# Later shifts, scales and gates beside the second norm, and another order of the exact split, in a two-model fp32 kernel

## The reference, cut to what matters

```python
mod = silu(c) @ ada_w[l] + ada_b[l]          # the same with c_ctx for the context
sh1, sc1, g1, sh2, sc2, g2 = split(mod, 6)
h = rmsnorm(x) * (1 + sc1) + sh1
x = x + g1 * mixer(h)                        # attention (and pooling) and an output projection
h2 = rmsnorm(x) * (1 + sc2) + sh2            # "the second norm"
x = x + g2 * hier_moe(h2)                    # 32 experts, top 2 inside one of 4 groups
```

## Time and profile before

| | us |
|---|---|
| median of three runs | 2233.94 |
| the profiled execution | 2236.17 |
| its span | 2234.0 |
| TensorE busy in the span | 1944.3 (87%) |
| DVE, ACT, POOL busy | 629.4, 375.3, 332.6 |
| share of the chain that ended last: TensorE, DMA | 56%, 31% |

### The profile page before, as it was taken

One profiled execution on the slowest core, in us unless ns is written; L12 is line 12 of the kernel. 1 busy time (PEld: TensorE's weight loads), 2 busy tenths in 40 slices (PEclk: granted clock), 3 DMA queues, 4 the chain that ended last, 5 costly groups with the idle time before them and its releaser, 6 DMA issues.

```text
span 2234.0 us, 32318 instructions
## 1 busy us (share of the span) xinstructions
PE 1944.3 (87%) x14055; PEld 1216.9 (54%) x14055; DVE 629.4 (28%) x1428; ACT 375.3 (17%) x807; POOL 332.6 (15%) x270
## 2 busy tenths in 40 slices
PE   5999969998988766999969988888849999988898
PEld 3577455655555434455645544444427767665784
DVE  1334342221211214123441111111136032035852
ACT  3143320000000003022231100000011130031131
POOL 0124430000000000013421000000002050040130
PEclk8999979999999997999969999999979999999999
DMA  9358229999999979125649999999964414426221
GB/s 364 117 203 307 77 111 423 424 426 424 425 426 425 425 286 316 42 87 183 217 169 383 424 421 425 424 422 423 423 258 152 155 55 151 151 76 190 76 87 57
DMA packets 138838, 593.48 MB, mean 266 GB/s; under 512 B 19316, under 2 KB 30612, under 8 KB 104768
## 3 DMA queue, kind: packets, MB, share of 16 engines
q1 hardware_dynamic: 113168, 557.86, 62.7%
q10 hardware_dynamic: 19344, 27.03, 3.6%
q0 software_dynamic: 6176, 6.42, 0.8%
HBM read 581.67 MB, written 21.65 MB: 270 GB/s over the span
## 4 chain that ended last, share of the span: by engine, by line
PE 56%; DMA 31%; DVE 5%; issue 3%; ACT 2%; POOL 2%; ACTq 0%; SPq 0%; POOLq 0%; DVEq 0%
DMA RG<-in_moe_w 29%; PE banks L1248 9%; PE banks L2111 8%; PE banks L2113 4%; PE banks L980 4%; PE banks L1683 3%; PE banks L592 3%; PE banks L1273 3%; PE banks L1685 3%; PE banks L2312 2%; PE banks L2509 2%; PE banks L1230 2%; PE banks L332 2%; PE banks L722 2%; PE banks L750 2%
## 5 line engine op out<-in xcount | busy, mean ns | idle before, releaser
L1248 PE MATMUL banks<-RG,HT 128*64 128x256 f32 x3744 | 426.7, 381 | 73.3 <-DMA RG<-in_moe_w 71.1
L1248 PEld LDWEIGHTS banks<-RG,HT 128*64 128x64 f32 x3744 | 262.2, 137 | 248.5 <-DMA RG<-in_moe_w 116.4
L1390 POOL DMA_INDIRECT y_rows<-AR x66 | 64.5, 978 | 895.4 <-DVE AR L1287 895.4
L1257 DVE TENSOR_TENSOR AR<-AR,banks 128x256 f32<-128x256 f32 x66 | 39.7, 602 | 540.5 <-ACT AR L1253 490.7
L1273 PE MATMUL banks<-RG,AR 128*64 128x512 f32 x768 | 175.4, 598 | 5.4 <-DVE AR L1266 3.6
L2111 PE MATMUL banks<-HT,RG 128*128 128x256 f32 x768 | 170.8, 384 | 0.7 <-ACT HT L468 0.7
L2111 PEld LDWEIGHTS banks<-HT,RG 128*128 128x128 f32 x768 | 147.3, 193 | 23.6 <-issue 2.4
L1253 ACT ACTIVATE AR<-banks 128x256 f32<-128x256 f32 x66 | 25.4, 384 | 773.4 <-PE banks L1248 773.4
L1230 PE MATMUL banks<-AR 128*128 128x256 bf16 x1152 | 149.4, 278 | 3.4 <-DVE AR L1219 3.4
L1230 PEld LDWEIGHTS banks<-AR 128*128 128x128 bf16 x1152 | 109.9, 100 | 38.7 <-issue 25.1
L461 PE MATMUL banks<-IDN,AR 128*128 128x128 f32 x144 | 29.0, 368 | 89.2 <-ACT AR L1630 29.9
(11 more groups left out here) (393 smaller groups left out, 2394.8 us busy)
## 6 DMA issues: line engine op xcount, KB each, us to landing
RG<-in_moe_w SPq DMA_DIRECT2D x165, 2048.0 KB, 25.9
AR<-in_moe_w SPq DMA_DIRECT2D x33, 2048.0 KB, 25.4
RG<-in_ada_w SPq DMA_DIRECT2D x24, 2048.0 KB, 9.1
RG<-in_attn_w_in SPq DMA_DIRECT2D x20, 2048.0 KB, 7.8
RG<-in_odd_w_in SPq DMA_DIRECT2D x6, 2048.0 KB, 17.8
RG<-in_ssm_w_in SPq DMA_DIRECT2D x4, 2048.0 KB, 9.1
AR<-y_rows ACTq DMA_DIRECT2D x6, 1024.0 KB, 8.1
RG<-in_even_w_in SPq DMA_DIRECT2D x2, 2048.0 KB, 22.8
```

Source lines behind the costliest of these rows:

```text
L1248: m = pe.matmul(p[64 * h:64 * h + 64, 256 * i:256 * i + 256], x[:, k, :], w[:, k, 256 * h:256 * h + 256], start=k == 0, stop=k == 7, skip_ ...
L1390: g.indirect_dma_start(y, off, E.Y[b], None, bounds_check=2047, oob_is_err=False).then_inc(*event)
```

## The change

The numbers computed are the same. The edits:

1. The six pieces that have late users, the odd layer's 0 to 3 and the even layer's 10 and 11, go out of the even attention; the odd layer's 10 and 11 go out of the odd attention (`ada_second` now ends at piece 9). In SP's order they stand behind the two pieces of the output projection and ahead of expert 0 (`LATE`). SP issues the odd layer's piece 3 only after the last gated product of the even layer ("gated", 0, 7), with a small load of the bias ahead of it.
2. Their row groups are made in `pe_project`: in the even layer two ahead of the last tile's turn, one between the turn (with the logits of the tile before) and the last tile's logits, three behind these; in the odd layer one ahead of the turn and one behind the logits. They write bank 3 (or 1) side by side.
3. In the routing DVE adds the biases (after the loads are counted), TensorE spreads the gates (16 instructions for each of two streams, or one, behind the ranks, on 64 partitions at a time so that both halves of the gate lie where they are used) and makes the four transposes, ACT moves the gates out with one copy each, and DVE moves the columns out behind "places". `act_gates` is gone.
4. The exact split: ACT makes part 0 ahead of the turned copies and part 1 right behind them and the store, so for a tile both now come before the next tile's squares. POOL makes the two rests between and behind the two residual additions of the next tile. The last tile's two rests are made by DVE, ahead of the routing.
5. In the root's refinement three operations of one element are written as `tensor_scalar` with the second operand as a per-partition scalar.
6. In the odd layer ACT issues two loads of constants (final_g, attn_pre_norm) behind the routing, where it issued them ahead of the projection.

```diff
+        LATE = ([(1, 0), (1, 1), (1, 2), (1, 3), (0, 10), (0, 11)], [(1, 10), (1, 11)])
...
-            for n in range(4, 12):
+            for n in range(4, 10):
                 cols(("ada", l, n), I["ada_w"][l], 512 * n, 512, ("ada_rows", l, n))
-            if l == 0:
-                for n in range(4):
-                    cols(("ada", 1, n), I["ada_w"][1], 512 * n, 512, ("ada_rows", 1, n))
             for n in range(2):
                 cols(("wo", l, n), I[("even_w_out", "odd_w_out")[l]][0], 512 * n, 512, ("po", l, 3 - 2 * l, n))
+            for a, n in LATE[l]:
+                cols(("ada", a, n), I["ada_w"][a], 512 * n, 512, ("ada_rows", a, n))
...
-        AB1 = ar(9 * KK, 4, 128)
+        AB1 = SVF[:, 0:512].rearrange("p (a b) -> p a b", a=4)
+        ABL = (ar(5 * KK, 2, 128), AB[:, 10:12])
...
-            return ada_steps(l, range(4, 12), (0, 1) if l == 0 else (0,), (7,), (7,))
+            return ada_steps(l, range(4, 10), (0, 1) if l == 0 else (0,), (7,), (7,))
...
+        def pe_late_rows(pe, l, i):
+            a, n = LATE[l][i]
+            bank = 3 if l == 1 or i < 4 else 1
+            before = ("gated", l, 2 if l == 1 else (5 if bank == 3 else 6))
+            pe_ada_rows(pe, a, n, bank, before, i % 4)
+
+        def dve_late_raw(v, l):
+            if l == 0:
+                v.wait_ge(*at("ab1_load"))
+                v.wait_ge(*at("ada_rows", 1, 3))
+                v.tensor_tensor(AB1, PS[3].rearrange("p (a b) -> p a b", a=4), AB1, ADD).then_inc(*ev("ada_raw", 1, 3))
+            v.wait_ge(*at("late_bias" if l == 0 else "ab2_load"))
+            v.wait_ge(*at("ada_rows", l, 11))
+            v.tensor_tensor(ABL[l], PS[1 + 2 * l][:, 0:256].rearrange("p (a b) -> p a b", a=2), ABL[l],
+                            ADD).then_inc(*ev("ada_raw", l, 11))
+
+        def pe_late_spread(pe, l):
+            pe.wait_ge(*at("ada_raw", l, 11))
+            for s in range(2 - l):
+                r = PS[(2, 4)[s]]
+                for j in range(4):
+                    c = IDN[:, 32 * j + s:32 * j + s + 1].broadcast_to([128, 64])
+                    for h in range(2):
+                        m = pe.matmul(r[64 * h:64 * h + 64, 128 * j:128 * j + 128], c, ABL[l][:, h, :], start=True, stop=True,
+                                      skip_group_check=True)
+                m.then_inc(*ev("ada_spread", l, 11, s))
+
+        def act_late_spread(act, l):
+            for s in range(2 - l):
+                o = (mods0, mods1)[l][(5, s)][:, 0:512]
+                act.wait_ge(*at("ada_spread", l, 11, s))
+                act.activation(o, PS[(2, 4)[s]], ACT.Copy).then_inc(*ev("ada_plain", l, 11, s))
+
+        def pe_late_cols(pe, l):
+            if l == 0:
+                pe.wait_ge(*at("ada_raw", 1, 3))
+                for n in range(4):
+                    pe_ada_cols(pe, 1, n, AB1[:, n, :], 5, None, n)
+
+        def dve_late_cols(v, l):
+            if l == 0:
+                v.wait_ge(*at("ada_turned", 1, 3))
+                for n in range(4):
+                    dve_ada_cols(v, 1, n, 5, n)
...
-            vstep(v, v.tensor_tensor(u, y, y, MUL))
-            vstep(v, v.scalar_tensor_tensor(out=u, in0=u, scalar=-0.5, in1=s, op0=MUL, op1=MUL))
-            v.scalar_tensor_tensor(out=y, in0=u, scalar=1.5, in1=y, op0=ADD, op1=MUL).then_inc(*ev("rstd", name))
+            if n == 1:
+                vstep(v, v.tensor_scalar(u, y, y, None, MUL))
+                vstep(v, v.tensor_scalar(u, u, -0.5, s, MUL, MUL))
+                ins = v.tensor_scalar(y, u, 1.5, y, ADD, MUL)
+            else:
+                vstep(v, v.tensor_tensor(u, y, y, MUL))
+                vstep(v, v.scalar_tensor_tensor(out=u, in0=u, scalar=-0.5, in1=s, op0=MUL, op1=MUL))
+                ins = v.scalar_tensor_tensor(out=y, in0=u, scalar=1.5, in1=y, op0=ADD, op1=MUL)
+            ins.then_inc(*ev("rstd", name))
...
         def pe_even_between(pe):
             yield from pe_ada(pe, 0, ada_second(0))
-            for n in range(4):
-                pe_ada_rows(pe, 1, n, 7, ("ada_cols", 1, n - 1) if n else spread_out(0, 11, 1))
-                yield
-                pe_ada_cols(pe, 1, n, MB[:, n % 2, :], 7, None)
-                yield
...
-            e.wait_ge(*at("ada_cols", 1, 3))
-            e.wait_ge(*at("ada_plain", 0, 11, 1))
+            e.wait_ge(*at("ada_plain", 0, 7, 1))
+            e.wait_ge(*at("ada_scale", 0, 9, 1))
...
+            first, second = ((2, 3), (1, 1))[l]
+            for i in range(first):
+                pe_late_rows(pe, l, i)
             pe_second_norm(pe, E, nt - 1)
+            for i in range(first, second):
+                pe_late_rows(pe, l, i)
             pe_logits(pe, E, nt - 1)
+            for i in range(second, len(LATE[l])):
+                pe_late_rows(pe, l, i)
 
...
-                if t:
-                    act_split(act, E, t - 1)
             act_second_norm(act, E, E.nt - 1)
-            act_split(act, E, E.nt - 1)
 
         def act_second_norm(act, E, t):
             act_root(act, (E.name, t), at_=t)
+            act.wait_ge(*at(norm_end(E.name, t), E.name, t))
+            act.activation(E.HB[t][:, 0], by_k(E.H[t]), ACT.Copy).then_inc(*ev("part0", E.l, t))
             act_turn(act, E.name, t)
-            act.wait_ge(*at(norm_end(E.name, t), E.name, t))
             act.dma_start(H2D[128 * t:128 * t + 128, :], E.H[t]).then_inc(*dm("h_store", E.l, t))
-            act.activation(E.HB[t][:, 0], by_k(E.H[t]), ACT.Copy).then_inc(*ev("part0", E.l, t))
+            act_split(act, E, t)
...
+        def rest(E, i, t):
+            return f"rest{i}_dve" if t == E.nt - 1 else f"rest{i}"
+
+        def rest_first(e, E, t):
+            e.wait_ge(*at("part0", E.l, t))
             if t:
-                g.wait_ge(*at("rest1", E.l, t - 1))
-            g.tensor_tensor(E.R, by_k(E.H[t]), E.HB[t][:, 0], SUB).then_inc(*ev("rest0", E.l, t))
-            g.wait_ge(*at("rest0", E.l, t))
-            g.wait_ge(*at("part1", E.l, t))
-            g.tensor_tensor(E.HB[t][:, 2], E.R, E.HB[t][:, 1], SUB).then_inc(*ev("rest1", E.l, t))
+                e.wait_ge(*at(rest(E, 1, t - 1), E.l, t - 1))
+            e.tensor_tensor(E.R, by_k(E.H[t]), E.HB[t][:, 0], SUB).then_inc(*ev(rest(E, 0, t), E.l, t))
+
+        def rest_second(e, E, t):
+            e.wait_ge(*at(rest(E, 0, t), E.l, t))
+            e.wait_ge(*at("part1", E.l, t))
+            e.tensor_tensor(E.HB[t][:, 2], E.R, E.HB[t][:, 1], SUB).then_inc(*ev(rest(E, 1, t), E.l, t))
 
         def dve_project(v, E):
             for t in range(E.nt):
@@ -1048,6 +1104,8 @@
                     v.tensor_tensor(E.tmp[h], PS[(1, 2, 3)[n % 3]], E.gate(t)[:, 512 * h:512 * h + 512],
                                     MUL).then_inc(*ev("gated", E.l, n))
             dve_second_norm(v, E, E.nt - 1)
+            rest_first(v, E, E.nt - 1)
+            rest_second(v, E, E.nt - 1)
...
-                if t:
-                    pool_split(g, E, t - 1)
+                    if t:
+                        (rest_first, rest_second)[h](g, E, t - 1)
             t = E.nt - 1
             pool_norm(g, E.name, t, like(E.H[t], E.mods[(3, t // 2)]), E.mods[(3, t // 2)])
-            pool_split(g, E, t)
...
             ins.then_inc(*ev("loads_counted", l))
+            dve_late_raw(v, l)
...
             v.tensor_reduce(E.rk, E.B4, AX, ADD).then_inc(*ev("places", l))
+            dve_late_cols(v, l)
...
+            act_late_spread(act, E.l)
...
+            pe_late_spread(pe, E.l)
+            pe_late_cols(pe, E.l)
...
-        def act_gates(act, l):
-            for g in ((mods0[(5, 0)], mods0[(5, 1)]), (XS[:, 3, :],))[l]:
-                ins = act.activation(g[64:128, 0:512], g[64:128, 512:1024], ACT.Copy)
-            ins.then_inc(*ev("gate_laid", l))
...
-                    v.wait_ge(*at("gate_laid", l))
+                    v.wait_ge(*at("ada_plain", l, 11, 1 - l))
...
-            act.dma_start(FG, rows(I["final_g"])).then_inc(*dm("final_loads", 0))
-            act.dma_start(PG1, rows(I["attn_pre_norm_2"][0])).then_inc(*dm("final_loads", 1))
             act.dma_start(OHT[0:32], K["k_oh"]).then_inc(*dm("dist_loads", 0))
             act.dma_start(RB2[0:32], I["rel_bias_2"]).then_inc(*dm("dist_loads", 1))
             act_project(act, E1)
             act_route(act, E1)
+            act.dma_start(FG, rows(I["final_g"])).then_inc(*dm("final_loads", 0))
+            act.dma_start(PG1, rows(I["attn_pre_norm_2"][0])).then_inc(*dm("final_loads", 1))
             act_experts(act, E1, act_dist)
...
-                    sp.wait_ge(*at("rest0", l, (3, 1)[l]))
+                    sp.wait_ge(*at("rest0_dve", l, (3, 1)[l]))
                     sp.wait_ge(*at("h_store", l, (3, 1)[l]))
                     sp.wait_ge(*at("logits", l, (3, 1)[l]))
+                if key == ("ada", 1, 3):
+                    sp.wait_ge(*at("gated", 0, 7))
+                    sp.dma_start(ABL[0], I["ada_b_pad"][0][:, 10:12]).then_inc(*dm("late_bias"))
```

(12 more changed lines are left out.)

29 lines of the change are left out of this document (11 added, 18 removed).

## The result

The changed kernel takes 2213.55 us (median of 4, 2211.22 to 2218.64) against 2233.2 for the kernel before beside it: ratio 0.9915, 95% interval 0.9903 to 0.9926. It is faster, and the time lies within the range given, but only 20 of the forecast 30 us came. On the profiled executions the span fell from 2234.0 to 2211.5, by 22.5 us.

What follows compares the result with a forecast made beforehand. The even experts' end was taken as their DMA stream's start plus a fixed time, delayed by TensorE-bound stages and tail. Savings 14 + 5.2 + 5 + 5.5 = 29.7 us gave 2206.5 profiled, 2204 on the median's scale; range 2194 to 2219.

Steps and rivals of the forecast that it cites:

- Even attention, 14: Even attention, steps 9 to 15: without inserted work each takes 2.2 us, saving 14 us (bounds 7 and 16.8).
- The norm, 4.6: Second norm of the last tile, both tails: the new exact split has it normed 4.6 us earlier.
- Even tail, 5.2: Even norm, routing and first selection: DMA engines limit, piece 7 at 323.4 against 328.63, saving 5.2 us (bounds 7 and -2.5).
- The nine pieces: Even tail: nine weight pieces of 4.95 us, 44.6 us in all, go between the fourth late piece's issue and piece 7.
- the three late groups beside the routing: Even tail: the last three late row groups on TensorE lie beside DVE's routing of 9.4 us.
- Odd attention, 5: Odd attention: four of 29 inserted items and a 0.62 us wait go, saving 5 us (bounds 3 and 6.6).
- Odd tail, 5.5: Odd norm, routing and selection: earlier norm and routing, logits at half clock, saving 5.5 us (bounds 3 and 10).
- A: Even attention: the ring of engines holds steps at 3.3 us, saving 7 instead of 14; 2211 us, chance 0.2.
- B: Even tail: the half clock stays throughout, piece 7 goes out 2.5 us later than before; 2212 us, chance 0.1.
- D: Even and odd tails: the slot ring makes pieces serial at 9.1 us each, 13 us slower; 2247 us, chance 0.05.
- C: Both tails: the clock stays full, so the odd tail gains 10 us; 2200 us, chance 0.1.
- E: Attention: its length is set by something outside TensorE's queue, nothing to be seen; 2234 us, chance 0.05.

Runs made afterwards that it cites:

- e5: Kernel before with only the new exact split and the new form of the small steps, no late pieces; ratio 0.9957 to the kernel before.
- e9: The changed kernel measured once more, nothing altered; ratio 0.9905 to the kernel before, median 2214.9 us.
- e10: Changed kernel with the odd layer's two late pieces back in its attention and both constant loads at the head of the odd stage; 2218.51 us.
- e1: Changed kernel with the slot table's indirect stores issued a second time, into a spare table nobody reads; ratio 0.9942 to the kernel before.
- e7: Changed kernel with the slot table's stores issued twice, the second set's elements dropped by a bound of 0; ratio 0.9900 to the kernel before.
- e6: Changed kernel with SP, in the even layer, holding the ninth queued weight piece until the slot table's eighth store is complete; ratio 0.9915 to the kernel before.
- e3: Changed kernel with SP's wait for the last gated product and the bias load two pieces further back; even projection to experts' read-back 609.8 us against 615.8.
- the six executions named with e10: Profiled executions of the changed kernel, e2, e3, e6, e7 and e9, all with odd late pieces; odd projection to end 1126.4 us on average.
- e2: Changed kernel with DVE's wait for the slot table moved from behind expert 0's h to behind expert 1's; ratio 0.9903 to the kernel before.
- e11: Changed kernel with the odd layer's late pieces back in attention, both constant loads at the stage's head, and the earlier stream start of e3; 2212.94 us.

## Why the prediction was right or wrong

**Even attention, 14: right.** It was 15.4 (14.3 to 16.0 over the traces with these pieces). The step was sized well: from step 9 on the scores are 2.26 us apart on average (179.71 to 193.27), 2.2 taken, and from step 9's scores to P0 14.3 us are saved (35.4 before, 21.1 now). The other 1.1 is ahead of step 9, which starts at 179.71 instead of 180.77; the forecast has no term for it. **The norm, 4.6: right,** 5.0 in both layers, and with the routing's 1.3 exactly the 5.9 of e5. On the small steps the prediction rightly followed the trace: the Trainium skill (SBUF — State Buffer, the part on which operations grab the shared pair) says that a tensor_scalar can enter a two-port mode and then contends with GpSimd; here they took 0.21 us each, two of the three wholly inside POOL's operation of 2.14, and did not wait.

**Even tail, 5.2: wrong, it was -0.5** (-0.4 and -0.7 in e9 and e10). The failed step is the sentence that ends the term: piece 7 at 323.4 against 328.63, "against 328.63 this is 5.2 us". It takes the rest of the stage as a fixed time behind piece 7, a rule read off a kernel whose stream stood still when the slot table was stored. The nine pieces were counted well: piece 7 found its queue still full. (Its issue is no measure of the gain. It came 9.2 us early in one trace and 4.0 in the other, and it stands 7.2 us behind the first expert's first matmul before, 3.7 and 8.6 in the two.) What was counted nowhere is what else uses the DMA engines in the newly filled time: POOL's eight indirect stores, 1024 elements of 4 bytes. Where the text came to the slot table it asked only whether it was late ("needed 7 us later - at nothing"), and not what its stores do to the stream. The runs showed 5.1 us lost in the changed kernel, 4.8 by e1 for a set that nobody waits for, at most 0.5 for a dropped set (e7), and the whole gain coming through without a stream (e5). 5.2 - 5.1 leaves 0.1; the measured -0.5 is within what two executions differ by. That the loss equals the gain is chance. No run took the stores out of the stream's way for nothing (e6 paid for it with the stream), so that the 5.2 would then have come is argued, not shown. The range's upper end took this term at 5, though the term's own bounds went down to -2.5; with that bound it would have ended at 2223.5.

**The last late piece.** I had the three late groups beside the routing, hidden. The last landed so late that TensorE stood for it and did it at half clock (0.54 granted in 283.13 to 286.60):

```profile
283.13 3.49 PE L335 MATMUL banks<-RG,SC 128*32 128x128 f32 x64 [3.39 <-DMA RG<-in_ada_w]
```

The ranks waited for it, not for DVE: 3 us on TensorE's path. As the stream, not TensorE, set the end, these should have cost little, which was not run by itself; e3 took them away together with the late start.

**Odd attention, 5: about right,** 3.9 (3.2 on e9). **Odd tail, 5.5: too high,** 3.7 and 1.6 in the two executions of the changed kernel, and 3.8 on average over the six executions named with e10 (1.6 to 6.1). The split brought 6.4 (e5), more than the 5.9 summed, and the clock was kinder than assumed:

```profile
1120.00:1129.00 9.00, 8.71 (x44) 8.65 (x48) 3.85 (x8) 5.39 (x5) 0.00 (x0) 0.50 0.84 348
```

The logits ran at 0.50, as in the earlier trace rows, and as forecast; the late group behind them (3.64 us) was followed by a selection at 0.92 granted, 5.87 us for its 48 matmuls where it took 8.12 at 0.65 before. The piece that waits for the first slot was issued 8.7 us early (63.2 us behind P1, before 72.0), against 5.2 forecast; some 5 of it were lost again behind it, where the table's stores meet the stream (10.16 us to completion).

**The rivals.** A, B and D are excluded by the scores' distance, the full clock in the even selection, and SP's issues 5 us a piece. C's full clock came in the even selection and nearly (0.92) in the odd one, not in the odd logits; E would have left P0 where it was. None of the rivals named the stores. The total came near A's 2211 for another reason, and it is inside the range although one of the four terms brought nothing.

## What to carry to other kernels

When a change fills a stretch in which the DMA engines stood idle, list every DMA that ran there unseen, small ones above all: here 1024 stores of 4 bytes, free before, took 5 us from a stream of 2 MB pieces (e1, e7). A stream's end is its start plus a fixed time only as long as nothing else moves into it. And a long wait of an engine that has its next work queued (TensorE's 3.78 us) proves nothing until it is taken away: e2 did, and won nothing. The same kernel's second trace had this wait at 1.39 us and was no faster: where two traces of one kernel are at hand, look at both before explaining a wait.

## What the runs showed of the hardware

Small indirect stores and a full weight stream hurt each other both ways. Eight stores of 128 elements of 4 bytes cost the stream 5.1 us (the changed kernel) and 4.8 (e1); four lengthened P1 to end by 1.4 to 3.5, which is at the edge of that stretch's scatter. Behind the end of its issue the last store is complete after 1.5 to 1.7 us with no stream (before, e5), 2.1 to 2.8 with little (the odd tails of e10 and e11, the even one of e6), and 4.9 to 11.0 with a full one (8.0 and 10.2 in the changed kernel). In the packet records of the changed kernel the stream's 16 KB packets take 0.61 us each, and those that start in 304 to 306 us 2.0 on average and up to 4.6, while the stores' own packets, of 32 bytes, are shown with 15 ns, all but three of 128. The same number of elements dropped by the bound costs at most 0.5 us of stream (e7, 410 GB/s against 422), and the experts' indirect stores of whole rows, six of them between 326 and 388 us, go beside a stream of 423 GB/s. The Trainium skill (DMA: Bandwidth & Descriptors, Specifications) says that transfers under 512 bytes are done as read-modify-write; that agrees with which of the stores hurt, but no run here shows the mechanism. The Trainium skill (DMA: Bandwidth & Descriptors, Queues, rings and completion order) says that each DMA engine takes packets from its queues in turn. That alone would leave the stream nearly all of the time and its packets at 0.61 us; the trace disagrees on the second, with packets of up to 4.6 us.
